# Both softmax attentions of a fused two-block kernel: packed values in two passes, other PSUM banks, other fill tables, tails among the slabs of the next phase

## The reference, cut to what matters

```
scores = q @ k.T                      # 512 x 512, causal by blocks of 128
p   = exp(scores - bias)              # A: distance slopes and window; B: mask of the chosen keys
o   = (p @ v) / sum(p)
o   = o * silu(g)                     # B only; A's result goes through w_attn_out and a gate
y   = o @ w_out
```

## Time and profile before

| what | value |
|---|---|
| median of 3 runs | 1651.69 us (1646.33 to 1653.17) |
| the profiled execution's own time | 1649.88 us |
| its span | 1648.1 us, 19418 instructions |
| mean granted clock of TensorE | 0.984 |
| busy: TensorE, VectorE, ScalarE, GpSimd | 1561.9, 886.0, 504.5, 546.1 us |
| HBM | 153 GB/s over the span |
| weights, issue to landing (median) | W_HI 3.9 us, W_LO 5.7 us |
| last chain, by engine | TensorE 86%, VectorE 5%, DMA 3%, ScalarE 3% |

### The profile page before, as it was taken

The page is one execution under the profiler, slowest core; times in us unless marked ns, Lnnn a source line. Parts: engine busy times, 40 slices in busy tenths (PEclk is TensorE's granted clock), DMA queues, the critical chain, the costliest instruction groups (busy, mean ns, idle before and its releaser), DMA issues.

```text
span 1648.1 us, 19418 instructions
## 1 busy us (share of the span) xinstructions
PE 1561.9 (95%) x7634; PEld 1273.9 (77%) x7634; DVE 886.0 (54%) x1546; ACT 504.5 (31%) x1001; POOL 546.1 (33%) x662
## 2 busy tenths in 40 slices
PE   6999999899899999999999999999998989999997
PEld 5878888677778778888878787687776768888885
DVE  2899949256645144333400031895676261677675
ACT  4223333356541132222200011311676130444440
POOL 3222234311114344444444444144110334332321
PEclk9999999999999999999999999999999999999999
DMA  8989998623338978898888888398321758755655
GB/s 227 193 184 194 195 191 188 153 66 63 77 77 183 225 169 193 191 198 190 196 172 192 184 176 194 78 189 182 77 52 26 164 120 193 156 123 117 140 109 145
DMA packets 69274, 253.12 MB, mean 154 GB/s; under 512 B 7616, under 2 KB 7744, under 8 KB 69184
## 3 DMA queue, kind: packets, MB, share of 16 engines
q0 software_dynamic: 66528, 242.25, 68.7%
q1 hardware_dynamic: 2112, 7.53, 1.3%
q10 hardware_dynamic: 544, 2.10, 0.4%
HBM read 249.75 MB, written 2.10 MB: 153 GB/s over the span
## 4 chain that ended last, share of the span: by engine, by line
PE 86%; DVE 5%; DMA 3%; ACT 3%; issue 2%; POOL 0%; SPq 0%; DVEq 0%; ACTq 0%; POOLq 0%
PE PSUM L451 26%; PE PSUM L452 25%; PE PSUM L453 25%; DMA W_LO<-wstream 2%; PE PSUM L612 2%; PE PSUM L633 2%; PE PSUM L714 1%; PE PSUM L732 1%; PE PSUM L745 1%; PE PSUM L600 1%; DVE MASK L1747 1%; DMA SMALLS<-small 1%; DMA W_HI<-wstream 1%; PE PSUM L643 1%; ACT PROBS L968 0%
## 5 line engine op out<-in xcount | busy, mean ns | idle before, releaser
L439 POOL DMA_DIRECT2D W_HI<-wstream x231 | 129.5, 561 | 946.8 <-PE PSUM L453 946.3
L451 PE MATMUL PSUM<-X_HI,W_HI 128*128 128x512 f32 x872 | 350.0, 401 | 5.7 <-DVE X_LO L1332 2.6
L452 PE MATMUL PSUM<-X_LO,W_HI 128*128 128x512 f32 x872 | 342.1, 392 | 0.0
L453 PE MATMUL PSUM<-X_HI,W_LO 128*128 128x512 f32 x872 | 342.0, 392 | 0.0
L433 POOL DMA_DIRECT2D W_LO<-wstream x231 | 208.0, 900 | 105.2 <-POOL W_LO L430 84.2
L451 PE MATMUL PSUM<-W_HI,X_HI 128*128 128x512 f32 x544 | 213.8, 393 | 7.0 <-DMA W_LO<-wstream 2.7
L430 POOL TENSOR_SCALAR W_LO<-W_HI 128x1024 fp32r<-128x1024 f32 x195 | 210.3, 1079 | 23.1 <-DMA W_HI<-wstream 19.6
L452 PE MATMUL PSUM<-W_LO,X_HI 128*128 128x512 f32 x544 | 212.8, 391 | 0.0
L453 PE MATMUL PSUM<-W_HI,X_LO 128*128 128x512 f32 x544 | 212.7, 391 | 0.0
L451 PEld LDWEIGHTS PSUM<-X_HI,W_HI 128*128 128x128 f32 x872 | 165.0, 189 | 44.8 <-issue 7.5
L453 PEld LDWEIGHTS PSUM<-X_HI,W_LO 128*128 128x128 f32 x872 | 164.7, 189 | 35.8
(11 more groups left out here) (225 smaller groups left out, 2465.8 us busy)
## 6 DMA issues: line engine op xcount, KB each, us to landing
W_HI<-wstream POOLq DMA_DIRECT2D x231, 512.0 KB, 3.9
W_LO<-wstream POOLq DMA_DIRECT2D x231, 512.0 KB, 5.7
GATE_A<-x SPq DMA_DIRECT2D x4, 512.0 KB, 5.8
GATE_B<-x SPq DMA_DIRECT2D x1, 2048.0 KB, 16.5
NORM_GAINS<-lnv ACTq DMA_DIRECT2D x2, 1024.0 KB, 5.9
out<-GATE_B SPq DMA_DIRECT2D x3, 512.0 KB, 2.6
CONST<-consts SPq DMA_DIRECT2D x1, 968.0 KB, 10.7
out<-GATE_B SPq DMA_DIRECT2D x2, 256.0 KB, 2.0
```

Of the source, the lines that this page charges most:

```text
L439: pool.dma_start(W_HI[:, n % SLOTS, :], wstream[n]).then_inc(w_hi_in[n % SLOTS], 16)
L451: pe.matmul(o, lh, rh, start=start, stop=False)
L452: pe.matmul(o, lh, rl, start=False, stop=False)
L453: return pe.matmul(o, ll, rh, start=False, stop=stop)
```

## The change

**Packed values.** One buffer ATT_V takes the place of V_HI and V_LO; they are now the two halves of it, as in C. Values are two passes into two banks (one for each head), followed by `low_products` on ScalarE and `both_parts` on VectorE; `output` then reads ATT_LOW instead of PSUM. The filling with zeros goes.

**Banks.** Scores have only banks 0 and 1, so scores(i, q) waits for biased(i, q-1). Values have 2 and 3, turned weights 4 and 5, the slab 6, and turned queries and keys 7, which queries and keys use in turn (`turn_qk(i + 1, 0)` at step 1, `turn_qk(i + 1, 1)` behind the values). Pair 0, the first slab and the last pair take banks that are free there.

**Fill tables.** B no longer has two slabs ahead of the attention; both tables put quarters at steps 0, 1 and 3.

**Order on the other engines.** The inverse is made behind biased(i, 0), `inverse_gate` comes ahead of PT_LO of block 3, PT_LO of blocks 0 and 1 behind biased(i, 3). The sums have a buffer for each parity of the pair.

**Heads and tails.** At the start of A and B the turning of pair 0 and two quarters stand ahead of the wait for the last tiles of the phase before. The last turnings and values stand among slabs: in A behind two more quarters each, with attn_out's first two slabs computed up to k = 6 ahead of the wait for the last pair (`attention_out`); in B among the first slabs of out_a (`out_a`). The activation tables for the exponential and for C's sigmoid are loaded earlier by a dummy instruction.

```diff
-SCORE_BANK, TURN_BANK, SLAB_BANK, OUT_BANK = ((0, 1), (2, 3)), (4, 5), 6, 7
+SCORE_BANK, OUT_BANK, TURN_BANK, SLAB_BANK, QK_BANK = (0, 1), (2, 3), (4, 5), 6, 7
+FIRST_QK_BANK = dict(a=(QK_BANK, TURN_BANK[1]), b=SCORE_BANK)
+FIRST_SLAB_BANK = dict(a=SLAB_BANK, b=OUT_BANK[1])
+LAST_OUT_BANK = dict(a=OUT_BANK, b=(SLAB_BANK, QK_BANK))
...
-A_EARLY, B_EARLY = 4, 2
-A_FILL = 2 * [[2, 2, 0, 2], [2, 0, 2, 2], [0, 2, 2, 0]] + [[2, 2, 0, 2], [2, 0, 0, 0]] + [[4, 4]]
-B_FILL = [[1, 1, 1, 1], [0, 1, 1, 1], [1, 0, 1, 1], [1, 1, 0, 1], [1, 1, 1, 0], [1, 1, 1, 1], [0, 0, 1, 0], [0, 1, 0, 0]] + [[2, 0]]
+A_EARLY = 4
+A_FILL = [[4, 2, 0, 2]] + 2 * [[2, 2, 0, 2], [2, 2, 0, 2], [1, 1, 0, 2]] + [[1, 1, 0, 2]] + [[2, 2]]
+B_FILL = [[3, 1, 0, 2]] + (PAIRS - 2) * [[1, 1, 0, 2]] + [[1, 1, 0, 0]]
...
+                    after(pe, f"{a}_qk_lo", 2 * i + j if i else 0)
...
-                    after(pe, f"{a}_biased", 2 * (4 * i + q) - 2)
+                    after(pe, f"{a}_biased", 2 * (4 * i + q))
...
-                            mm = mm3(PSUM[:, OUT_BANK, kb * P:], V_HI[:, kb, h, :], V_LO[:, kb, h, :],
...
+                            for part in (PT_HI, PT_LO):
+                                mm = pe.matmul(PSUM[:, out_bank(a, i)[h], kb * P:], ATT_V[:, kb, h, :],
+                                               part[:, h, r, :].rearrange("p b q -> p (b q)"),
+                                               start=kb == 0 and part is PT_HI, stop=kb == TT - 1 and part is PT_LO)
...
-                turn_qk(0)
+                turn_qk(0, 0)
+                turn_qk(0, 1)
+                fill(0, 0, slice(2))
+                pe.wait_ge(tile_free, t0)
...
+                    if i < PAIRS - 1:
+                        turn_qk(i + 1, 0)
                     fill(i, 1)
                     scores(i, 2)
-                    fill(i, 2)
-                    if i < PAIRS - 1:
-                        turn_qk(i + 1)
                     if i:
                         values(i - 1)
-                    scores(i, 3)
+                    if i < PAIRS - 1:
+                        turn_qk(i + 1, 1)
                     turn_p(i, 0)
                     turn_p(i, 1)
+                    scores(i, 3)
                     fill(i, 3)
...
+                pe.wait_ge(sem("a_biased"), 8 * PAIRS)
+                for n in range(2):
+                    slab_ready(s0 + n)
+                    part(n, range(KT - 1))
+                for n in range(2):
+                    part(n, (KT - 1,)).then_inc(slab_done, 1)
...
+                pe.wait_ge(sem("b_biased"), 8 * PAIRS)
+                pe.wait_ge(sem("b_add"), 2 * PAIRS - 2)
+                t_half(0, s0, KT, O_HI, O_LO, TILE0["g2"] + 1, ready, slabs=(0,))
+                last_scores()
+                t_half(0, s0, KT, O_HI, O_LO, TILE0["g2"] + 1, ready, slabs=(1,))
+                last_values()
+                t_half(0, s0, KT, O_HI, O_LO, TILE0["g2"] + 1, ready, slabs=(2, 3))
...
+                def low_products(i):
+                    after(act, f"{a}_pv", i + 1)
+                    after(act, f"{a}_o", i)
                     for h in range(2):
...
+                        d, other = slice(h * HD, (h + 1) * HD), slice((1 - h) * HD, (2 - h) * HD)
+                        act.activation(ATT_LOW[d, :], PSUM[other, out_bank(a, i)[h], :], ACT.Copy).then_inc(sem(f"{a}_low"), 1)
...
+                def both_parts(i):
+                    for h in range(2):
+                        d = slice(h * HD, (h + 1) * HD)
+                        after(dve, f"{a}_low", 2 * i + h + 1)
+                        dve.tensor_tensor(ATT_LOW[d, :], PSUM[d, out_bank(a, i)[h], :], ATT_LOW[d, :], ALU.add)\
+                            .then_inc(sem(f"{a}_add"), 1)
...
-                    dve.scalar_tensor_tensor(QKV[:, 1, :, o_part(i)], PSUM[:, OUT_BANK, :].rearrange("p (t q) -> p t q", q=P),
+                    dve.scalar_tensor_tensor(QKV[:, 1, :, o_part(i)], ATT_LOW[:, :].rearrange("p (t q) -> p t q", q=P),
```

More of the change, by code:

```diff
@@ L686, in softmax_attention, with last_scores, attention_out, part @@
                     turn_p(i, 1)
+                    scores(i, 3)
                     fill(i, 3)
                 turn_p(PAIRS - 1, 2)
+                def last_scores():
+                    turn_p(PAIRS - 1, 3)
+                    turn_inverse(PAIRS - 1)
+                return last_scores, lambda: values(PAIRS - 1), fill
+            def attention_out(last_scores, last_values, fill):
+                s0, t0 = SLAB0["attn_out"], TILE0["attn_out"]
+                def part(n, ks):
+                    s = (s0 + n) % SLOTS
+                    for k in ks:
+                        w = slice(k * P, (k + 1) * P)
+                        pe.wait_ge(sem("a_ol"), k + 1)
+                        mm = mm3(PSUM[:, n, :], W_HI[:, s, w], W_LO[:, s, w], O_HI[:, :, o_part(k)], O_LO[:, :, o_part(k)],
+                                 k == 0, k == KT - 1)
+                    return mm
@@ L947, in attention @@
-            def attention(a, sq, sk, name, table, early):
-                s0 = SLAB0[name]
-                def qk_hi(i):
-                    for j, s in enumerate((sq, sk)):
-                        after(act, f"{a}_turned", 2 * i + j + 1)
-                        after(act, f"{a}_scores", 4 * i - 4)
-                        act.activation(QK_HI[:, i % 2, j, :], PSUM[:, TURN_BANK[j], :], ACT.Copy, scale=s)\
-                            .then_inc(sem(f"{a}_qk_hi"), 1)
+                for n in halves:
+                    i, c = n // 2, n % 2
+                    act.wait_ge(slab_done, s0 + 4 * n + 4)
+                    for t in range(TT):
+                        dst = QKV[:, bass.ds(i + j0, 1), t, c * SEQ:(c + 1) * SEQ]
+                        bank = (first_bank + 4 * c) % 8 + t
+                        act.activation(dst, PSUM[:, bank:bank + 1, :], ACT.Copy).then_inc(tile_free, 1)
@@ new lines, in load_exp_table, with attention, qk_hi @@
+            def load_exp_table():
+                act.activation(warm[:, :], zero[:, :], ACT.Exp).then_inc(sem("warmed"), 1)
+            def attention(a, sq, sk, name, table, begun=None):
+                s0 = SLAB0[name]
+                def qk_hi(i, j):
+                    after(act, f"{a}_turned", 2 * i + j + 1)
+                    after(act, f"{a}_scores", 4 * i - 4)
+                    act.activation(QK_HI[:, i % 2, j, :], PSUM[:, qk_bank(a, i, j), :], ACT.Copy, scale=(sq, sk)[j])\
+                        .then_inc(sem(f"{a}_qk_hi"), 1)
@@ L1012, in gate @@
                         after(act, "b_gated", n)
-                        bank = OUT_BANK if early and n == 1 else SLAB_BANK
-                        act.activation(GATE_TANH[:, 0, :], PSUM[:, bank, :], ACT.Tanh, scale=0.5).then_inc(sem("b_gate"), 1)
+                        act.activation(GATE_TANH[:, 0, :], PSUM[:, slab_bank(a, n), :], ACT.Tanh, scale=0.5).then_inc(sem("b_gate"), 1)
                 def gates(i, q):
@@ L1018, in gates @@
                         gate(n)
-                for buf in (V_HI, V_LO):
-                    for h in range(2):
-                        d = slice((1 - h) * HD, (2 - h) * HD)
-                        act.activation(buf[:, :, h, d], zero[:, 0:1].unsqueeze(2).to_broadcast([P, TT, HD]), ACT.Copy)\
-                            .then_inc(sem(f"{a}_v_zero"), 1)
-                if early:
-                    gate(0)
-                qk_hi(0)
-                if early:
-                    gate(1)
+                qk_hi(0, 0)
+                qk_hi(0, 1)
+                if begun:
+                    begun()
                 for i in range(PAIRS):
-                    last = i == PAIRS - 1
                     if i:
@@ L1421, in gate @@
                         after(dve, "b_gate", n + 1)
[L1422 to L1423 removed]
+                        dve.scalar_tensor_tensor(GATE_A[:, n, :], GATE_TANH[:, 0, :], 1.0, PSUM[:, slab_bank(a, n), :],
+                                                 ALU.add, ALU.mult)\
                             .then_inc(sem("b_gated"), 1)
```

225 lines of the change are left out of this document (110 added, 115 removed).

## The result

| | before | after |
|---|---|---|
| median | 1652.26 us (1646.33 to 1653.17, 4 runs) | 1599.39 us (1597.64 to 1603.88, 4 runs) |
| the profiled execution's own time | 1649.88 us | 1597.64 us |
| its span | 1648.1 us | 1595.8 us |
| mean granted clock of TensorE | 0.984 | 0.991 |
| W_LO, issue to landing (median) | 5.7 us | 5.6 us |

The account below looks back on a forecast made before the run. TensorE, busy 95% of the span, was taken as the bound. 1648.1 - 21.8 + 2.4 - 34.2 - 15.7 + 15.1 = 1593.9 us of span, with 1.8 added 1595.7: forecast 1596 us, range 1580 to 1622.

Parts of the forecast that it names:

- Waits and clock of the old order: First and second attention: all 34.2 us of TensorE's idle time and 15.7 us of lower clock are removed.
- The ruler: A pair of the second attention without TensorE waits, 14.73 us with three quarters, used to price both attentions.
- New waits: Waits that the new order adds in both attentions, +15.1 us in sum, bounds 0 and 50.
- (1): Last pair of the second attention: without a quarter at step 3, turn_p 2 waits for PT_LO, 2.5 us.
- (2): Head of the second attention: the third quarter waits for ScalarE's four copies behind two QK_HI, 0.6 us.
- (3): First attention, step 3: GpSimd's negation stretches output and head_bias where six slabs end, 6 x 1.0 us.
- (4): First attention: three pairs with four quarters, where VectorE also makes head_bias, 1.0 us each.
- The weight stream: attn_out's first slab is released 4 us later; four slabs loaded ahead are 20 us of work, so nothing.
- The tightest place: VectorE between scores 1 and the values: 3.4 us of work against 4.0 on TensorE, holds by 0.6 us.
- rival (b): Both attentions: VectorE as hidden bound comes late at values and scores 3: 1630.5 us, half of it 1605.6; chance 0.15.
- Rival (c): Each of 20 slabs of both attentions: GpSimd stretches a VectorE instruction by 1.1 us, TensorE waits: 1612 us; chance 0.10.
- Rival (d): Single scores bank in both attentions: each of 64 blocks costs TensorE 1.05 + 0.69 us: 1692 us; chance 0.03.

Follow-up runs that it names:

- the run with the tables alone: The kernel before, with only the new fill tables of both attentions: 1634.55 us, ratio to the kernel before 0.9882.
- the run in plain order: The changed kernel with attn_out's first two slabs in plain order, each released when its eighth K tile is done: 1598.82 us.
- the run with the moved quarter: The changed kernel with one quarter of the second attention moved from step 3 of pair 6 to step 3 of pair 7: 1600.11 us.
- GpSimd held: The changed kernel, where GpSimd waits for head_bias before it issues and negates at slabs ending at step 3 of the first attention: 1592.29 us.
- ScalarE negating: The changed kernel, where ScalarE in place of GpSimd negates twelve slabs of weights during the first attention: 1591.98 us.
- the three edits together: The changed kernel with GpSimd held back until head_bias, attn_out in plain order and one quarter moved to the second attention's last pair: 1589.66 us.

## Why the prediction was right

The forecast was 1596 us, and 1599.39 was measured; of the span, 1593.9 and 1595.8. Of all its rivals none took place as a whole. By its steps:

- **Values in two passes**, -21.8: the values take 2.61 us (2.60 forecast), and a third pass put back costs 21.8 by the medians and 1.3 us a pair. Shown.
- **Waits and clock of the old order**, -34.2 and -15.7: the granted clock is 1.00 in A and B, and for PT_LO and QK_LO together TensorE waits 3.3 us in the whole kernel. More than half of the gain beside the passes comes from the tables (19 of some 31 us), as the run with the tables alone shows.
- **The ruler**: 14.8 us for B's pairs, 14.92 measured; VectorE 12.6 and 12.5, ScalarE 11.5 and 11.8. The prediction says that the ruler explains both old stretches; in B it leaves 3.4 us of the 150 unexplained (146.6). The sum of one undisturbed pair carried the whole forecast.
- **New waits**, +15.1: the sum is met (14.9), but by luck: a term that I had put at nothing, 5.4 us for the weight stream, fills what others left. (1) B's tail 2.31 (2.5 forecast). (2) B's head 0.2 (0.6), and for QK_LO, not for the copies. (3) GpSimd's negation, 4.7 us (6), by four meetings and not six that reach TensorE. (4) The pairs with four quarters, 1.3 (3). (5) Small waits, 3: 1.0 in A, and no clock in the profiled execution.
- **The weight stream, "so nothing"**: this step failed. W_LO is waited for 5.4 us more. I took four slabs loaded ahead as four slabs of slack for the late release of attn_out's first slab. But GpSimd issues the low load of a slab only behind the high load of the next one, so three slabs stand ahead of it, and two releases at once put the loads in a queue. 2.0 of the 5.4 us are this, by the run in plain order. The rest is not traced to an edit. The 1.6 us in w_out are there with the new tables alone (4.3 in all), but gone with the third pass over the values (2.4), and the 1.6 in out_a mostly go in runs that touch nothing near it (3.0 down to 1.7), so part of both belongs to the single execution. The DMA engines are busy for 0.93 of the time in w_out (window 505 to 545 of the changed kernel), but for 0.96 at the same place of the kernel before (535 to 575), so a fuller stream is not what changed.
- **The tightest place** was put between scores 1 and the values, with 0.6 us. It is at the other end of the step: copies, additions, biased 3, scores 0 of the next pair, with 0.2 to 0.4 us. How much is left at the place that I named no run measured. The forecast did not suffer, since the chain holds; but rival (b), VectorE as the hidden bound, was nearer than its 0.15 says. Two more instructions on each of the two engines at this place brought 1.9 us a pair.
- **Rival (c)**, every slab of A and B: in B no instruction is stretched: beside all eight negations at the ends of its slabs VectorE reads the scores of 384 columns (0.55 us) and a gate (0.68), both from PSUM, and takes as long as elsewhere. What happened is the forecast's mild form. The Trainium skill, "SBUF — State Buffer", section "Who interferes with whom", has a VectorE instruction with two inputs in SBUF and a GpSimd instruction that reads SBUF exclude each other for a whole instruction; output against the negation agrees (2.03 us against 0.68), and so does output against a bare issue of a load, which reads no tensor (0.68).
- **Rival (d)**, the single scores bank: it is what TensorE waits for in all 6.0 us of A, of which 4.7 go with GpSimd's negation; in B's middle pairs it costs nothing.

## What to carry to other kernels

Measure one undisturbed repetition of the inner loop, price a quarter and a change of operands from it, and write each stage as that sum plus waits plus clock: what the sum leaves over is what a new order can win. Look for slack at the places where one engine's order carries a chain to the bound engine, not in shares of busy time: 2.4 us of free time in a pair were worth 0.2 to 0.4 us at the place that mattered. And where one queue carries two loads of each slab in turn, count the look-ahead for the later of the two.

## What the runs showed of the hardware

- The granted clock behind one and the same wait differs from run to run. Pair 6 of A holds a wait of 2.0 us in the changed kernel and in the run with the moved quarter. Windows of that pair, first the changed kernel:

```profile
412.81:430.10 17.29, 15.26 (x98) 11.87 (x98) 14.46 (x35) 12.36 (x32) 2.54 (x3) 1.00 0.30 62
```

```profile
415.26:434.17 18.91, 16.86 (x97) 13.40 (x97) 14.54 (x35) 12.36 (x32) 2.53 (x3) 0.91 0.27 57
```

  One is granted the full clock and the other 0.91, for 1.6 us. With GpSimd held, that wait is 0.65 us long and the four runs lie within 1.1 us of each other (1591.69 to 1592.83), at a mean clock of 0.991 or 0.992; the changed kernel's four lie within 6.2 us, at 0.985 to 0.991. But ScalarE negating and the three edits together have the same short wait and spread by 5.4 and 5.8 us, and attn_out in plain order has the long one and spreads by 3.1. So what makes the spread is not shown.
- In the four meetings of output and the negation, VectorE's row starts 0.42 us ahead of GpSimd's and yet ends 0.54 us behind it (360.45 + 2.03 against 360.87 + 1.07). GpSimd's row is as long as elsewhere (1.07 us); VectorE's, which starts first, carries the whole delay. So the order of the starts in the profile does not tell which of the two will wait.
- Copies and additions over 64 partitions cost what 128 cost: 0.59 us for a copy (PT_HI of 128 partitions 0.60) and 0.69 for an addition (QK_LO of 128 partitions 0.69), means over B's pairs 1 to 6 for 512 columns each, as in the earlier trace rows.
